# Memory handed over with its features on the partitions, no identity turns ahead of the first product, and the first two weight panels advanced together by contraction tiles

## The chip, the cores and the metric

The kernel runs on one core of a Trainium2 chip. The metric is device time in microseconds (us) of that core, for one execution of the whole block. The engines are named as in the profile: PE multiplies matrices, ACT, DVE and POOL work element by element, SP issues most transfers (DMAs).

## The reference, cut to what matters

The block normalises an input `x` (512 tokens, 1024 features) and runs three mixer branches. Only the opening of the third, the attention into 256 memory tokens, and what lies beside it are touched here:

```python
mem_h = rms_norm(mem, mem_norm_g[l])            # mem: 256 tokens x 1024 features
kv_m = mem_h @ w_mem_kv[l]                      # 1024 x 2048, four panels of 512 columns
km = rms_norm(kv_m[..., :D_MEM].reshape(B, -1, MEM_HEADS, MEM_HD), mem_k_norm_g[l])
vm = kv_m[..., D_MEM:].reshape(B, -1, MEM_HEADS, MEM_HD)
...
h = rms_norm(x, norm_g[l])
proj = h @ w_in[l]
```

All of it is fp32; a product needs its contraction (the features) on the partitions.

## The kernel before, in words

Every fp32 operand is split into a high part (rounded) and a low part (the rest), and each product is three matmuls: high by high, high by low, low by high. ACT makes the high parts (`w_hi`, `memT_hi`), DVE the low parts (`w_lo`, `memT_lo`), PE multiplies. Three engines thus follow each other for each weight piece: `piece_high` (L1234) on ACT, `piece_low` (L1859) on DVE, `first_products` (L780) on PE.

The opening works on panels 0 and 1 of `w_mem_kv`, each 8 contraction tiles (k = 0 to 7, 128 rows each) by 512 columns, for two memory tiles m of 128 tokens: 2 x 2 x 8 x 3 = 96 matmuls of 512 columns, into four PSUM banks `proj0` to `proj3`. `w_raw`, `w_hi` and `w_lo` hold two halves (kh 0 and 1) of four contraction tiles. `PIECES` (L26) cuts the loads: panel 0's tiles 0 to 3 one by one (pieces 0 to 3), panel 1's tiles 0 to 3 in two pairs (4, 5), panel 0's tiles 4 to 7 in two pairs (6, 7, into the same place as pieces 0 to 3). The rest comes by `load_kv_half` (L434). Pieces 6 and 7 wait on SP for `w_lo_done` 1, the low part of piece 3, and on ACT for `w_used` 1, the last product of the tiles that they replace.

The memory comes with tokens on partitions (`load_mem`, L452, four transfers of 256 KB). PE turns each half of a memory tile with the identity (`turn_tile`, L663, four turns of 128 x 128), ACT writes the high part out of PSUM times the gain (`mem_high`, L1209) and DVE the low part (`mem_low`, L1833). The gain is loaded as rows on ACT's queue and turned too (L777). `warm` (L769) fills PE's start with identity turns. A product of a memory tile waits for the tile's turn and split, so `first_products` takes one panel and one memory tile after the other in an order written out by hand (L793 to L815).

The sums of squares of the memory come from ACT's `square` (L1197) with an accumulating output; `variance` on DVE and a power on POOL (L2544) make 1/rms, and `kv_evac` (L1265) applies it when ACT takes the banks out of PSUM. After panels 0 and 1 PE runs panel 2 (`kv_panel`, L746) into banks 0 and 1, with the turns of `x` between its products, then a turn of 92 rows of small vectors (`vector_transposes`, L684), then the rest of the block. SP's queue is one list: pieces, then `load_kv_half` with the four tiles of `x` between, then small vectors, then `w_in`.

Each engine takes its instructions in the order written; a wait holds all that stands behind it on that engine.

Of the kernel before, what the change touches and what calls it, by code (L numbers as in the profile page):

```python
# [7 lines left out]
F32 = mybir.dt.float32  # L8
# [6 lines left out]
P = 128  # L15
# [13 lines left out]
FIRST_BANKS = ((0, 1), (2, 3))  # L29
WARM_TURNS = (8, 7)  # L30
# [111 lines left out]
def hybrid_block(nc, x, mem, positions, norm_g, mem_norm_g, w_in, conv_w, conv_b, mlstm_gate_b,  # L142
                 mlstm_norm_g, dsa_q_norm_g, dsa_k_norm_g, mem_q_norm_g, mem_k_norm_g,
                 w_mem_kv, w_branch, w_out, inv_freq, pos_cols, w_idx2, out):
    ctx = ExitStack()
    with ctx:
# [44 lines left out]
        mem_in = merged[:, 0:MT * D].rearrange("p (t n) -> p t n", t=MT)  # L191
        g_row = arena[:, 0:D]
        memg_rows = arena[0:KT, D:D + P]
        memg_col = cols[:, 0:KT]
        x_sc = arena[:, 2 * D:4 * D].rearrange("p (b n) -> p b n", b=2)
        junk = arena[:, 4 * D:5 * D]
        idx2_raw = arena[:, 8 * D - KT * I_COLS:8 * D].rearrange("p (k n) -> p k n", k=KT)
        vec_rows = arena[0:92, 5 * D:5 * D + P]
# [130 lines left out]
        mem_landed = [sem(f"mem_landed{n}") for n in range(2 * MT)]  # L329
        g_landed, memg_landed = sem("g_landed"), sem("memg_landed")  # L330
        mem_hi = sem("mem_hi")
        half_turned, half_hi, half_lo = sem("half_turned"), sem("half_hi"), sem("half_lo")
# [52 lines left out]
        vec_cols = sem("vec_cols")  # L385
        memg_cols = sem("memg_cols")
# [9 lines left out]
        def turn_bank(n, k):  # L396

            return att[FIRST_BANKS[n][k // 2] if n < MT else TURN_BANK[n]]

        def half_tile(n):  # L400

            return (n % 2, n // 2) if n < 2 * MT else (n // 2, n % 2)

# [4 lines left out]
        wi, wkv, wo = w_in[0], w_mem_kv[0], w_out[0]  # L408
# [15 lines left out]
        def _(sp):  # L424
# [9 lines left out]
            def load_kv_half(n, p, c0, kh):  # L434

                for i, free, landed in ((0, (w_first_lo, n + 4), piece_landed[n]), (1, (w_lo_done, p * 2 + kh - 1), w_landed[kh])):
                    sp.wait_ge(*free)
                    rows = slice(kh * S + i * 256, kh * S + (i + 1) * 256)
                    sp.dma_start(w_raw[:, kh, 2 * i:2 * i + 2], wkv[rows, c0:c0 + 512].rearrange("(k p) n -> p k n", p=P))\
                        .then_inc(landed, 16)  # L440
# [38 lines left out]
            load_kv_half(0, KV_PANEL[1], 512, 1)  # L479
            load_x(X_TILES[:2])  # L480
# [2204 lines left out]
```

## Time and profile before

| | |
|---|---|
| median of 3 runs | 976.26 us (976.03 to 976.55) |
| span of the profiled execution | 974.9 us |
| busy share of the span: PE, DVE, ACT, POOL | 100%, 67%, 53%, 25% |
| moved by DMA | 103.36 MB |

A timeline row is: start (us from the span's start), duration, engine, line, operation, output<-inputs, shape, count of merged instructions, and in brackets the idle time of the engine ahead of it with what ended it. Matmul ends are modelled and overlap the next start, so the distance of starts tells the pace. A row of the windows gives, for a stretch, the busy time and count of each engine, the granted clock, the mean busy share of the DMA engines and what they moved in GB/s.

### The profile page before, as it was taken

Reading aid. Unit: us, or ns where it says so; the run is one execution under the profiler, and the core shown is the slowest. Engines: PE = TensorE matmul, PEld = TensorE weight load, DVE = VectorE, ACT = ScalarE, POOL = GpSimd, SP = SyncE. Lnnn points to the kernel's source line nnn. Section 1 sums busy time; section 2 is a strip of 40 time slices with the busy share of each in tenths; the row PEclk is TensorE's granted clock in tenths of the full one; section 3 lists DMA queues with packets and bytes.
Section 4 is the critical chain, followed back from the end, with each engine's and each line's share of the span. In section 5 each row is a group of like instructions: output and inputs, shape, how many; then the busy total and the mean of one; then the engine's idle time right before and its main releaser. Section 6 shows DMA issues by size and latency. Waiting matters only on the chain.

```text
span 974.9 us, 13868 instructions
## 1 busy us (share of the span) xinstructions
PE 970.7 (100%) x4993; PEld 857.5 (88%) x4993; DVE 649.9 (67%) x1047; ACT 518.5 (53%) x790; POOL 246.0 (25%) x167
## 2 busy tenths in 40 slices
PE   9999999999999999999999999999999999999998
PEld 7888888898989989989898888898998989988887
DVE  6878987779565564653756443796776867735486
ACT  6977644445453453544447211776675857741351
POOL 0100822121011010010110800271622626106600
DMA  8624222112332322332322342707024050638412
GB/s 277 242 87 130 87 87 76 45 54 68 95 97 65 97 65 78 84 95 66 97 87 87 87 129 76 237 12 213 4 80 146 31 153 1 229 94 302 153 43 87
DMA packets 111622, 103.36 MB, mean 106 GB/s; under 512 B 4468, under 2 KB 95192, under 8 KB 111196
## 3 DMA queue, kind: packets, MB, share of 16 engines
q1 hardware_dynamic: 111564, 102.80, 33.5%
q8 instruction: 26, 0.43, 0.2%
q14 instruction: 16, 0.13, 0.0%
q10 hardware_dynamic: 16, 0.00, 0.0%
HBM read 98.59 MB, written 4.20 MB: 105 GB/s over the span
## 4 chain that ended last, share of the span: by engine, by line
PE 100%; POOL 0%; issue 0%; DVE 0%; POOLq 0%
PE proj L619 59%; PE proj L1064 9%; PE att L1091 7%; PE proj L1091 5%; PE att L1141 3%; PE proj L789 2%; PE att L946 2%; PE att L964 2%; PE att L886 1%; PE att L908 1%; PE proj L1021 1%; PE att L954 1%; PE att L935 1%; PE att L679 1%; PE att L1021 1%; PE proj L1141 1%
## 5 line engine op out<-in xcount | busy, mean ns | idle before, releaser
L1807 DVE TENSOR_TENSOR w_lo<-w_raw,w_hi 128x1536 fp32r<-128x1536 f32 (+1 forms) x58 | 124.0, 2138 | 134.8 <-ACT w_hi L1191 129.5
L1191 ACT ACTIVATE w_hi<-w_raw 128x1536 fp32r<-128x1536 f32 (+1 forms) x58 | 97.4, 1680 | 147.9 <-PE proj L619 147.7
L619 PE MATMUL proj<-hT_hi,w_hi 128*128 128x512 f32 x384 | 150.2, 391 | 0.0
L619 PE MATMUL proj<-hT_hi,w_lo 128*128 128x512 f32 x384 | 149.8, 390 | 0.0
L619 PE MATMUL proj<-hT_lo,w_hi 128*128 128x512 f32 x384 | 149.6, 390 | 0.0
L619 PE MATMUL proj<-w_hi,hT_hi 128*128 128x384 f32 (+1 forms) x280 | 96.7, 345 | 0.0
L619 PE MATMUL proj<-w_hi,hT_lo 128*128 128x384 f32 (+1 forms) x280 | 95.3, 340 | 0.0
L619 PE MATMUL proj<-w_lo,hT_hi 128*128 128x384 f32 (+1 forms) x280 | 95.1, 340 | 0.0
L619 PEld LDWEIGHTS proj<-hT_hi,w_lo 128*128 128x128 f32 x384 | 72.1, 188 | 15.2
L619 PEld LDWEIGHTS proj<-hT_lo,w_hi 128*128 128x128 f32 x384 | 72.1, 188 | 14.5
L619 PEld LDWEIGHTS proj<-hT_hi,w_hi 128*128 128x128 f32 x384 | 72.1, 188 | 14.5
L619 PE MATMUL proj<-y_hi,w_hi 128*128 128x512 f32 x192 | 75.4, 393 | 0.0
L619 PE MATMUL proj<-y_lo,w_hi 128*128 128x512 f32 x192 | 74.8, 389 | 0.0
L619 PE MATMUL proj<-y_hi,w_lo 128*128 128x512 f32 x192 | 74.7, 389 | 0.0
L2574 POOL TENSOR_TENSOR arena<-arena 128x1024 f32<-128x1024 f32 x8 | 15.2, 1896 | 229.9 <-ACT arena L1466 229.9
L619 PEld LDWEIGHTS proj<-w_hi,hT_hi 128*128 128x128 f32 x280 | 52.6, 188 | 1.4
L619 PEld LDWEIGHTS proj<-w_lo,hT_hi 128*128 128x128 f32 x280 | 52.6, 188 | 1.4
L619 PEld LDWEIGHTS proj<-w_hi,hT_lo 128*128 128x128 f32 x280 | 52.5, 188 | 1.0
L2299 DVE TENSOR_TENSOR w_lo<-w_raw,w_hi 128x1536 fp32r<-128x1536 f32 (+1 forms) x21 | 35.3, 1682 | 23.4 <-ACT w_hi L1593 23.4
L2605 POOL TENSOR_TENSOR w_raw<-merged,w_raw 128x384 f32<-128x384 f32 x32 | 41.9, 1351 | 29.8 <-DVE w_lo L2299 29.8
L1593 ACT ACTIVATE w_hi<-w_raw 128x1536 fp32r<-128x1536 f32 (+1 forms) x21 | 29.1, 1387 | 31.4 <-POOL w_raw L2605 12.9
L619 PEld LDWEIGHTS proj<-y_hi,w_lo 128*128 128x128 f32 x192 | 36.0, 188 | 7.5
(445 smaller groups left out, 2399.3 us busy)
## 6 DMA issues: line engine op xcount, KB each, us to landing
w_raw<-w_in_in SPq DMA_DIRECT2D x106, 256.0 KB, 3.2
w_raw<-w_in_in SPq DMA_DIRECT2D x32, 512.0 KB, 4.4
w_raw<-w_in_in SPq DMA_DIRECT2D x6, 1024.0 KB, 5.3
w_raw<-w_mem_kv_in SPq DMA_DIRECT2D x10, 512.0 KB, 7.2
yF<-x_in SPq DMA_DIRECT2D x8, 512.0 KB, 7.9
w_raw<-w_branch_in SPq DMA_DIRECT2D x16, 256.0 KB, 3.5
w_raw<-w_branch_in SPq DMA_DIRECT2D x4, 1024.0 KB, 6.4
w_raw<-w_branch_in SPq DMA_DIRECT2D x8, 512.0 KB, 5.5
```

The costliest lines, as they stand in the source:

```text
L619: ins = mm(ps, lhs[a](k, k0), rhs[b](k, k0), start=(first and k == 0 and j == 0), stop=(last and k == KH - 1 and j == 2))
L789: ins = mm(banks[2 * c + m][:, :], memT[a][:, k, m * P:(m + 1) * P], (w_hi, w_lo)[b][:, c, k % KH, :], start=(k == 0 and j == 0), stop=(k ...
L946: ins = mm(att[(t + 2) % 4][:, 0:(t + 1) * P], b_qT[a][:, t * P:(t + 1) * P], b_kT[b][:, 0:(t + 1) * P], start=(j == 0), stop=(j == 2))
L964: ins = mm(att[2][:, s * P:S], v[:, s, :], b_pT[p][:, 4 * s * P:(3 * s + TT) * P], start=(s == 0 and j == 0), stop=(s == TT - 1 and j == 2))
L1064: ins = mm(banks[b][:, :], w[a][:, k, e * P:(e + 1) * P], hT[b_][:, kh * KH + k, :], start=(kh == 0 and k == 0 and j == 0), stop=(kh == 1 ...
L1091: ins = mm(to[t][:, 0:UNIT_N], lhs[a](k, t), w[b][:, k, :], start=(start and k == 0 and j == 0), stop=(k == KH - 1 and j == 2), skip_group ...
L1141: ins = mm(to[t][:, :], lhs[a](k, t), w[b][:, k, :], start=(start and k == 0 and (a, b) == (0, 0)), stop=(k == KH - 1 and (a, b) == parts[ ...
L1191: A_(w_hi[:, kh, :, 0:n], w_raw[:, kh, :, 0:n], ACT.Copy).then_inc(w_hi_done, 1)
L1593: A_(operand(op_hi, n), raw_of(n, first), ACT.Copy).then_inc(op_high, 1)
L1807: V.tensor_tensor(w_lo[:, kh, :, 0:n], w_raw[:, kh, :, 0:n], w_hi[:, kh, :, 0:n].bitcast(F32), ALU.subtract).then_inc(w_lo_done, 1)
L2299: V.tensor_tensor(operand(op_lo, n), raw_of(n, first), operand(op_hi, n).bitcast(F32), ALU.subtract)\
L2605: ins = G.tensor_tensor(dst[:, at], left[:, at], right[:, at], ALU.subtract)
```

## The change

- The host hands the memory over transposed, gain in front: `mem_t` is 128 partitions x (8 gains + 8 tiles x 256 tokens). Its first two contraction tiles are loaded on ACT's queue (132 and 128 KB), tiles 2 and 3 (256 KB) and 4 to 7 (512 KB) on SP's. `w_mem_kv` is handed over with each partition's rows of a panel in one piece, and the small vectors as columns (one load in place of five, no turn of them on PE).
- PE's turns of the memory and of the gain are gone. PE starts with one product of a constant tile and 14 identity turns. `mem_high` and `mem_low` work on one contraction tile of 256 tokens at a time, out of SBUF.
- `first_products` takes both memory tiles, and panels 0 and 1 advance together: one tile of each, the next tile of each, then pairs. The pieces are loaded in that order; piece 4 is now panel 0's tiles 2 and 3, and its low part is the `w_lo_done` 1 for which SP's load of piece 6 waits. One tile of `x` is queued ahead of that wait.
- Features lie on partitions now, so the sum of squares over features is a sum over partitions: ACT squares the memory in two parts (`mem_square`) after piece 7, POOL adds 2048 values per partition down to 256 in three steps, PE sums over the partitions with two one-column products (`mem_row_totals`), DVE and POOL make 1/rms of both memory tiles at once.

```diff
-TURN_BANK = (0, 1, 0, 1, 2, 3, 0, 1, 2, 3, 0, 1)
-PIECES = ((0, 0, 1), (0, 1, 2), (0, 2, 3), (0, 3, 4), (1, 0, 2), (1, 2, 4), (0, 0, 2), (0, 2, 4))
-LAST_PIECES = {3: 16, 5: 16, 7: 32}
+TURN_BANK = (2, 3, 0, 1, 2, 3, 0, 1)
+MEM_PIECES = ((0, 1), (1, 2), (2, 4), (4, 8))
+PIECES = ((0, 0, 1), (1, 0, 1), (0, 1, 2), (1, 1, 2), (0, 2, 4), (1, 2, 4), (0, 0, 2), (0, 2, 4))
+LAST_PIECES = {4: 16, 5: 16, 7: 32}
...
             load_piece(0, 0, 0)
-            load_mem(1)
-            load_piece(1, 0, 0)
+            load_piece(1, 0, 1)
             load_piece(2, 0, 0)
-            load_piece(3, 0, 0)
-            load_piece(4, 0, 512)
+            load_piece(3, 0, 1)
             load_mem(2)
-            load_piece(5, 0, 512)
+            load_piece(4, 0, 0)
+            load_piece(5, 0, 1)
             load_mem(3)
+            load_x(X_TILES[:1])
             sp.wait_ge(w_lo_done, 1)
             load_piece(6, 1, 0)
             load_piece(7, 1, 0)
...
+            def mem_row_totals():
+                pe.wait_ge(mem_summed, 1)
+                for m in range(MT):
+                    ins = mm(att[1][:, m:m + 1], mem_sq[:, m * P:(m + 1) * P], ones[:, :], start=True, stop=True)
+                ins.then_inc(mem_totals, 1)
...
+            pe.wait_ge(warm_set, 1)
+            mm(att[3][:, 0:P], warm_src, warm_src, start=True, stop=True)
             pe.wait_ge(ident_set, 1)
-            warm(WARM_TURNS[0])
-            pe.wait_ge(memg_landed, 16)
-            turn(att[2][:, 0:KT], memg_rows, ident[0:KT, 0:KT]).then_inc(memg_cols, 1)
-            turn_tile(0)
-            warm(WARM_TURNS[1])
+            warm(WARM_TURNS)
...
+            first_products(0, 0, 1, (w_first_cast, 1), (w_first_lo, 1), 1)
+            first_products(1, 0, 1, (w_first_hi, 1), (w_first_lo, 2), 1)
+            first_products(0, 1, 2, (w_first_hi, 2), (w_first_lo, 3), 2)
+            first_products(1, 1, 2, (w_first_hi, 3), (w_first_lo, 4), 2)
+            first_products(0, 2, 4, (w_hi_done, 1), (w_lo_done, 1), 4).then_inc(w_used, 1)
+            first_products(1, 2, 4, (w_hi_done, 2), (w_lo_done, 2), 4).then_inc(w_used, 1)
+            first_products(0, 4, 6, (w_first_hi, 4), (w_first_lo, 5), 6)
+            first_products(0, 6, 8, (w_hi_done, 3), (w_lo_done, 3), 8, (proj_done[0], proj_done[1]))
+            mem_row_totals()
+            first_products(1, 4, 6, (w_first_hi, 5), (w_first_lo, 6), 6)
+            first_products(1, 6, 8, (w_hi_done, 4), (w_lo_done, 4), 8, (proj_done[2], proj_done[3]))
...
+            act.dma_start(mem_in[:, 0:KT + MEM], mem_t[:, 0:KT + MEM]).then_inc(mem_landed[0], 16)
+            act.dma_start(mem_in[:, KT + MEM:KT + 2 * MEM], mem_t[:, KT + MEM:KT + 2 * MEM]).then_inc(mem_landed[1], 16)
...
             piece_high(6)
             piece_high(7)
-            square(0)
+            mem_square(0)
+            mem_square(1)
             half_high(1, 0, 2, (w_used, 2))
-            square(1)
             square(2)
             square(3)
...
             half_low(1, 0, 1)
-            variance(0)
-            variance(1)
+            mem_variance()
...
+            pool.wait_ge(mem_squared, 2)
+            steps.then(G.tensor_tensor(mem_sq[:, 0:D], mem_sq[:, 0:D], mem_sq[:, D:2 * D], ALU.add))
+            steps.then(G.tensor_tensor(mem_sq[:, 0:512], mem_sq[:, 0:512], mem_sq[:, 512:D], ALU.add))
+            G.tensor_tensor(mem_sq[:, 0:256], mem_sq[:, 0:256], mem_sq[:, 256:512], ALU.add).then_inc(mem_summed, 1)
```

PE before, in the second half of panels 0 and 1 (tiles 4 to 7): `proj0` and `proj1` are panel 0 for the two memory tiles, `proj2` is panel 1.

```order
L789 MATMUL proj0<-w_lo,y_hi 128x512 [waits w_lo_done]
L789 MATMUL proj0<-w_lo,y_hi 128x512
L789 MATMUL proj1<-w_hi,y_hi 128x512 [waits xT_lo]
L789 MATMUL proj1<-w_hi,y_lo 128x512 x4
L789 MATMUL proj1<-w_lo,y_hi 128x512 x4
L789 MATMUL proj2<-w_hi,y_hi 128x512 [waits w_first_hi]
```

PE now, at the same place, from the products of piece 7's low part on:

```order
L766 MATMUL proj0<-w_lo,y_hi 128x512 [waits w_lo_done,mem_high_of]
L766 MATMUL proj1<-w_lo,y_hi 128x512 x2
L766 MATMUL proj0<-w_hi,y_lo 128x512 [waits mem_low_of]
L766 MATMUL proj1<-w_hi,y_lo 128x512 x2
L665 MATMUL att1<-ones,arena 128x1 [waits mem_summed]
L665 MATMUL att1<-ones,arena 128x1
L766 MATMUL proj2<-w_hi,y_hi 128x512 [waits w_first_hi,mem_high_of]
```

Between panel 0's last product and panel 1's next one PE now has two one-column products that wait for POOL (`mem_summed`).

POOL before, from its opening on (`ident` and `causal` are constants, the rest is the power for 1/rms):

```order
L2533 MEMSET ident 128x128
L2534 AFFINE_SELECT ident<-ident 128x128
L2536 MEMSET causal 128x128
L2537 AFFINE_SELECT causal<-causal 128x128 [waits pool_step]
L2544 TENSOR_TENSOR small<-small,minus_half 128x1 [waits x_var,consts]
L2544 TENSOR_TENSOR small<-small,minus_half 128x1 [waits x_var] x5
```

POOL now, behind the same constants:

```order
L2483 AFFINE_SELECT causal<-causal 128x128 [waits pool_step]
L2489 TENSOR_TENSOR arena<-arena 128x1024 [waits mem_squared,consts]
L2490 TENSOR_TENSOR arena<-arena 128x512 [waits pool_step]
L2491 TENSOR_TENSOR arena<-arena 128x256 [waits pool_step]
L2493 TENSOR_TENSOR small<-small,minus_half 128x2 [waits x_var]
L2496 TENSOR_TENSOR small<-small,minus_half 128x1 [waits x_var] x4
```

Three additions, each waiting for the one before, stand ahead of the powers; the first waits for both squares of ACT.

DVE now, between piece 6 and the variance of the memory (L1815 are the low parts of pieces 6 and 7, L1828 those of panel 1's tiles 4 to 7):

```order
L1815 TENSOR_TENSOR w_lo<-w_raw,w_hi 128x1024 [waits w_first_hi]
L1815 TENSOR_TENSOR w_lo<-w_raw,w_hi 128x1024 [waits w_hi_done]
L1849 CAST small<-small 128x4 [waits ang_landed]
L1851 TENSOR_TENSOR arena<-arena,small 128x256 [waits dve_step]
L1853 TENSOR_SCALAR arena<-arena 128x256 [waits dve_step]
L1828 TENSOR_TENSOR w_lo<-w_raw,w_hi 128x1024 [waits w_first_hi,dve_step]
L1828 TENSOR_TENSOR w_lo<-w_raw,w_hi 128x1024 [waits w_hi_done]
L1785 TENSOR_SCALAR small<-att 128x2 [waits mem_totals]
```

Its order is that of before; the last row took the place of two single variances, and it waits for PE's totals where those waited for ACT.

## Rows read from the trace of the kernel before

**Rows 1.** The page: busy time of PE, and PE's 40 slices.
```profile
PE 970.7 (100%) x4993; PEld 857.5 (88%) x4993; DVE 649.9 (67%) x1047; ACT 518.5 (53%) x790; POOL 246.0 (25%) x167
PE   9999999999999999999999999999999999999998
```
**Rows 2.** Timeline of PE, start: identity turns and first products.
```profile
1.54 1.97 PE L772 MATMUL att<-ident 128*128 128x128 f32 x8 [1.54 <-POOL ident L2534]
...
5.97 0.78 PE L789 MATMUL proj<-w_hi,y_hi 128*128 128x512 f32 x1
6.54 0.63 PE L789 MATMUL proj<-w_lo,y_hi 128*128 128x512 f32 x1
6.97 0.63 PE L789 MATMUL proj<-w_hi,y_lo 128*128 128x512 f32 x1
```
**Rows 3.** Timeline of PE: panel 1's last 24 products, panel 2, the vectors' turn.
```profile
25.15 0.62 PE L789 MATMUL proj<-w_hi,y_hi 128*128 128x512 f32 x2
...
30.59 0.39 PE L619 MATMUL proj<-w_hi,y_hi 128*128 128x512 f32 x1
...
45.07 0.24 PE L687 MATMUL att<-ident,arena 92*128 92x92 f32 x1
45.38 0.43 PE L619 MATMUL proj<-hT_hi,y_hi 128*80 128x512 f32 x1
```
**Rows 4.** The windows: four stretches of the opening.
```profile
2.00:9.00 7.00, 7.00 (x30) 5.75 (x29) 3.31 (x10) 3.59 (x11) 0.08 (x1) 1.00 0.80 246
9.00:12.00 3.00, 3.00 (x14) 2.44 (x13) 1.99 (x6) 1.35 (x3) 0.00 (x0) 1.00 1.02 366
12.00:15.00 3.00, 3.00 (x16) 2.21 (x15) 1.37 (x2) 1.95 (x2) 0.00 (x0) 1.00 0.71 206
20.00:30.00 10.00, 10.00 (x46) 8.28 (x45) 8.72 (x20) 8.55 (x14) 3.23 (x4) 1.00 1.02 398
```
**Rows 5.** Timeline of ACT: high parts of pieces 4, 6 and 7, first square.
```profile
12.20 1.06 ACT L1242 ACTIVATE w_hi<-w_raw 128x1024 fp32r<-128x1024 f32 x1 [0.78 <-DMA w_raw<-w_mem_kv_in]
...
17.09 1.11 ACT L1242 ACTIVATE w_hi<-w_raw 128x1024 fp32r<-128x1024 f32 x1
18.36 1.06 ACT L1242 ACTIVATE w_hi<-w_raw 128x1024 fp32r<-128x1024 f32 x1 [0.16 <-DMA w_raw<-w_mem_kv_in]
19.32 1.04 ACT L1207 ACTIVATE arena<-merged 128x1024 f32<-128x1024 f32 x1
```
**Rows 6.** Timeline of DVE: low parts of pieces 3 and 4.
```profile
11.45 0.69 DVE L1865 TENSOR_TENSOR w_lo<-w_raw,w_hi 128x512 fp32r<-128x512 f32 x1 [1.01 <-ACT w_hi L1242]
13.29 1.23 DVE L1865 TENSOR_TENSOR w_lo<-w_raw,w_hi 128x1024 fp32r<-128x1024 f32 x1 [1.15 <-ACT w_hi L1242]
```
**Rows 7.** Timeline of all engines: SP's queue issues pieces 6 and 7.
```profile
12.17 0.89 SPq L459 DMA_DIRECT2D w_raw<-w_mem_kv_in  x2
```
**Rows 8.** Timeline of POOL: additions and subtractions of two SBUF operands.
```profile
111.64 1.30 POOL L2561 TENSOR_TENSOR arena<-arena 128x512 f32<-128x512 f32 x1 [0.18 <-ACT arena L1415]
112.89 4.47 POOL L2562 TENSOR_TENSOR y_hi<-yF,m_qh 128x1024 fp32r<-128x1024 f32 x1
...
140.14 2.41 POOL L2562 TENSOR_TENSOR y_hi<-yF,m_qh 128x1024 fp32r<-128x1024 f32 x1
...
553.74 2.40 POOL L2592 TENSOR_TENSOR arena<-arena 128x1024 f32<-128x1024 f32 x1
```
**Rows 9.** Timeline of DVE at two of those times.
```profile
112.81 2.29 DVE L1807 TENSOR_TENSOR w_lo<-w_raw,w_hi 128x2048 fp32r<-128x2048 f32 x1
...
547.05 4.36 DVE L1807 TENSOR_TENSOR w_lo<-w_raw,w_hi 128x2048 fp32r<-128x2048 f32 x1
```
**Rows 10.** Lines by shape, DVE, 0 to 50 us: low parts of two tiles.
```profile
L1878 DVE TENSOR_TENSOR w_lo<-w_raw,w_hi 128x1024 fp32r<-128x1024 f32 x6 | 7.2, 1224 | 1.4 <-ACT w_hi L1252 0.8 <-ACT w_hi L1254 0.5
```
**Rows 11.** Timeline of all engines: variance, power, evacuation of banks 0 and 1.
```profile
24.91 0.21 DVE L1822 TENSOR_SCALAR small<-small 128x1 f32<-128x1 f32 x2
25.21 1.19 POOL L2544 TENSOR_TENSOR small<-small,minus_half 128x1 f32<-128x1 f32 x2 [23.14 <-DVE small L1822]
...
29.13 1.25 ACT L1271 ACTIVATE merged<-proj,small 128x512 f32<-128x512 f32 x2
```

More of the change, by code:

```diff
@@ L496, in _ @@
             load(IDX_PANEL, [(wi, C_QI, 512)])
-            load(KV_PANEL[3], [(wkv, 3 * 512, 512)])
+            for kh in range(2):
+                sp.wait_ge(w_lo_done, KV_PANEL[3] * 2 + (kh - 1))
+                sp.dma_start(w_raw[:, kh], w_kv[:, 3, kh * KH:(kh + 1) * KH]).then_inc(w_landed[kh], 16)
             with sp.Fori(0, M_HEADS) as h:
@@ L772, in warm @@
                     turn(att[3][:, 0:P], ident[:, :], ident[:, :])
+            pe.wait_ge(warm_set, 1)
+            mm(att[3][:, 0:P], warm_src, warm_src, start=True, stop=True)
             pe.wait_ge(ident_set, 1)
-            warm(WARM_TURNS[0])
-            pe.wait_ge(memg_landed, 16)
-            turn(att[2][:, 0:KT], memg_rows, ident[0:KT, 0:KT]).then_inc(memg_cols, 1)
-            turn_tile(0)
-            warm(WARM_TURNS[1])
-            def first_products(c, m, k0, k1, high=(), low=(), mem_low=(), weights_last=True):
-                orders = (((0, 0), high), ((1, 0), mem_low), ((0, 1), low))
-                if not weights_last:
-                    orders = (orders[0], orders[2], orders[1])
-                for j, ((a, b), wait) in enumerate(orders):
-                    if wait:
-                        pe.wait_ge(*wait)
-                    for k in range(k0, k1):
-                        ins = mm(banks[2 * c + m][:, :], memT[a][:, k, m * P:(m + 1) * P], (w_hi, w_lo)[b][:, c, k % KH, :],
-                                 start=(k == 0 and j == 0), stop=(k == KT - 1 and j == 2))
-                return ins
@@ new lines, in first_products @@
+            def first_products(c, k0, k1, high, low, mem_ready, done=()):
+                for j, (a, b, wait) in enumerate(((0, 0, high), (0, 1, low), (1, 0, None))):
+                    pe.wait_ge(mem_low_of if a else mem_high_of, mem_ready)
+                    if wait is not None:
+                        pe.wait_ge(*wait)
+                    for m in range(MT):
+                        for k in range(k0, k1):
+                            ins = mm(banks[2 * c + m][:, :], memT[a][:, k, m * P:(m + 1) * P], (w_hi, w_lo)[b][:, c, k % KH, :],
+                                     start=(k == 0 and j == 0), stop=(k == KT - 1 and j == 2))
+                        if done and j == 2:
+                            ins.then_inc(done[m], 1)
+                return ins
@@ new lines, in square, with mem_square @@
+                act.wait_ge(x_landed[X_TILES[i - MT]], 16)
+                if i > MT:
+                    act.wait_ge(x_ssq, i - MT)
+                A_(junk, x_in[:, X_TILES[i - MT]], ACT.Square, accum_out=xss[:, i:i + 1]).then_inc(x_ssq, 1)
+            def mem_square(half):
+                for n in ((0, 1, 2), (3,))[half]:
+                    act.wait_ge(mem_landed[n], 16)
+                A_(mem_sq[:, half * D:(half + 1) * D].rearrange("p (k n) -> p k n", k=KH),
+                   memT_raw[:, half * KH:(half + 1) * KH], ACT.Square).then_inc(mem_squared, 1)
@@ L1286, in _ @@
             piece_high(3)
+            mem_high(2)
+            mem_high(3)
             piece_high(4)
             piece_high(5)
-            mem_high(2)
-            mem_high(3)
+            for k in range(KH, KT):
+                mem_high(k)
             piece_high(6)
             piece_high(7)
-            square(0)
+            mem_square(0)
+            mem_square(1)
             half_high(1, 0, 2, (w_used, 2))
-            square(1)
             square(2)
@@ L1892, in _ @@
             piece_low(3)
+            mem_low(2)
+            mem_low(3)
             piece_low(4)
             piece_low(5)
-            mem_low(2)
-            mem_low(3)
+            for k in range(KH, KT):
+                mem_low(k)
             piece_low(6)
```

270 lines of the change are left out of this document (96 added, 174 removed).

## The prediction

> **What bounds the kernel now.** I read the page first: PE is busy for 970.7 of 974.9 us, and its first slice of 24 us is as full as the others [rows 1]. So a change of this opening counts only by the moment at which PE can go on with the work that is the same in both kernels; nothing later is idle and could absorb a delay. That work is the last 24 products of panel 1 (its tiles 4 to 7), then panel 2 and the rest. In PE's timeline they start at 25.15 and panel 2 at 30.59, so 24 products take 5.44 us or 0.227 each, the 2.4 GHz level; the first products stand 0.43 apart (6.54 to 6.97), the 1.2 GHz level [rows 2, 3]. I then read the windows for what the loads reach [rows 4], and ACT, DVE, SP and POOL around the pieces and the sums [rows 5 to 11]. The sum below is for one number, the start of those 24 products now, against 25.15. The profiled run has a span of 974.9 us and the median of the runs is 976.26; I keep the 1.3 us outside the span.
>
> **What is removed.** The turns of the memory and the gain stand between products. Without them the first product can start behind 14 turns of 1.97/8 = 0.246 us from 1.54 on, at 4.98 at the earliest, instead of 5.97 [rows 2]. 72 products stand ahead of the last 24. With 6 at 0.43 and 66 at 0.227 they take 17.6 us, and PE would come to the 24 products at about 22.5 if nothing else made it wait: a gain of 2.65 us at the most. The vectors' turn costs 45.07 to 45.38, 0.31 us [rows 3]; it goes whatever else happens, since the columns come by a load long before they are used.
>
> **What is added: a wait in PE's order.** The two one-column products of the totals stand between panel 0's last product and panel 1's next. PE takes its work in order, so the 24 products, panel 2 and all behind them are queued behind a wait for POOL, which waits for ACT's squares, which stand behind the high part of piece 7 on ACT. Call the start of that high part L7 (18.36 in before [rows 5]). From there:
> - ACT: the high part holds ACT 0.96 (18.36 to 19.32), two squares take 0.96 and 1.04: 2.95 us [rows 5].
> - POOL: 1024 columns 2.40, 512 columns 1.30; for 256 no row exists, and half of the step from 512 to 1024 taken off 1.30 gives 0.75 as an estimate: 4.45 us [rows 8].
> - Three hand-overs between engines and the waits between POOL's steps 0.3, the two narrow products 0.2 (estimates; the vectors' turn took 0.31 [rows 3]).
>
> That is L7 + 7.9 us. POOL, however, doesn't run beside DVE here. The subtraction of two SBUF operands over 1024 columns takes 2.41 us on POOL alone and 4.47 when DVE's subtraction (2.29 us) began 0.08 us ahead of it; the other way round DVE's took 4.36 where POOL's 2.40 us addition was running [rows 8, 9]. One waits for the whole of the other. The Trainium skill, "SBUF — State Buffer", section "Who interferes with whom", says the same of a two-input DVE operation and GpSimd, and the trace agrees (4.47 for 2.41). In the new order of DVE the low parts of panel 1's tiles 4 to 7, two of 1.22 us [rows 10], become ready behind the squares, while POOL adds. If each takes its turn between two additions, POOL's chain grows by 2.44 to **L7 + 10.35**.
>
> **When L7 comes.** SP may load piece 6 only when piece 4's low part is done; before it was piece 3's. As many bytes stand ahead of piece 4 as ahead of it before (2052 against 2048 KB), so it may land near 12.2, where ACT took it [rows 5]. Its high part (1.06) and low part (1.23) then end at 14.5 [rows 5, 6], and SP issues pieces 6 and 7 at 14.55 instead of 12.17 [rows 7]. From the issue to the high part of piece 7 before went 18.36 - 12.17 = 6.2 us: upper end 20.7. Lower end: at the 398 GB/s of 20 to 30 us from 2 us on [rows 4], the 4.72 MB up to piece 7 would be there at 13.9; but ACT may write tiles 4 to 7 only after the 36th product, 4.98 + 2.6 + 30 x 0.227 = 14.4, and piece 6's high part stands ahead: 15.3. I take **18.4**, as before. The reason is the hole at 12 to 15 us: 206 GB/s where 398 are possible, so some 576 KB weren't moved while SP waited [rows 4]. The tile of `x` queued ahead of the wait (512 KB) fills just that, so piece 7's end moves little. Rows of the weights and the memory that are longer in DRAM may lift the 246 GB/s of 2 to 9 us [rows 4]; that counts to the lower end.
>
> **The sum.** With L7 at 18.4, piece 7's low part ends at 20.7 and 8 products of 0.227 behind it end panel 0 at 22.5. The squares end at 21.35, the additions at about 28.3, the totals at 28.75. PE stands idle for 6 us, and the 24 products start at 28.75 instead of 25.15: +3.6; less 0.31 for the vectors' turn: +3.3. 976.26 + 3.3 = **979.6 us** (span 978.2).
>
> **What costs nothing.** Behind the totals the variance, the power and the two evacuations (0.21, 1.19, 1.25 us [rows 11]) run beside the 24 products (5.44 us); without that cover panel 2 would wait for banks 0 and 1, up to 2.7 us. The `mem_high` and `mem_low` steps are fewer and wider than before, on engines that wait for loads at that time; if they delayed a piece they would move L7 within its bounds. The other two squares, the later loads of `x` and panel 2 go into the time at 398 GB/s in which PE has its 24 products and panel 2 ahead of it; the one load of columns replaces five.
>
> **The rivals.**
> - **The clock falls in the wait.** Before, the first products ran at the lower level although PE had been turning since 1.54, and reached 0.227 only behind 6.97 [rows 2]: coming out of no work costs some 5.4 us of lower level. After 6 us of nothing the 24 products may do so again. If it lasts 3.4 us (8 products) that is 8 x 0.2 = 1.6 us, if it lasts 6 us (14 products) 2.8: about 981.8. Against it speaks only that no row of before shows an idle PE in the middle, and that the idle time is shorter if the lock bites less. The Trainium skill, "TensorE: Matmul & The Clock Gate", section "Why this matters for your kernels", says that pauses between bursts of matmuls bring the half clock back; no row here shows it.
> - **Early pieces, lock as taken** (L7 15.3 to 17.4): the 24 products at 25.65 to 27.75, 976.5 to 978.6.
> - **The lock doesn't bite** (DVE's low parts come late, for lack of their weights, or early, before the additions), L7 as taken: 26.3, +1.15 - 0.31, about 977.1.
> - **Early pieces and no lock: faster.** This is the other side. The mechanism is the loads: four first pieces in the order in which they are used, and two queues, so that L7 comes near 15.3. Then the totals are there at 23.2, and the gain of the removed turns stays: 23.2 - 25.15 - 0.31 = -2.3, 974.0; at best 22.5, which gives 973.3. It decides for faster below L7 = 15.6 and needs DVE out of POOL's way; against it speaks the rate of 246 GB/s [rows 4].
> - **Late pieces** (L7 19.4 to 20.7, lock): 980.6 to 981.9.
>
> **How the numbers follow.** A measurement of this kernel can tell 0.2%, or 1.95 us, from no change: faster is below 974.3, slower above 978.2. Chances: the forecast (L7 17.4 to 19.4, lock, clock kept, 978.6 to 980.6) 0.29; the clock falls (980.6 to 983.0) 0.23; early pieces with lock 0.17, of which 0.03 above 978.2; no lock 0.11; early and no lock (973.3 to 975.7) 0.13, of which 0.09 below 974.3; late 0.07. Slower: 0.29 + 0.23 + 0.07 + 0.03 = 0.62. Faster: 0.09. Within: 0.29. The range leaves out the lower half of the faster case and the upper part of the clock's case: 974.5 to 982.6.
>
> **What would show it.** On PE, an idle time of 3 to 6 us that POOL's last addition ends, ahead of the two narrow products: right; none, and the 24 products at about 22.5: the wait is hidden and the forecast is wrong. On ACT, the start of piece 7's high part tells L7. On POOL, additions of 2.4, 1.3 and 0.75 us mean no lock; 2.5 or 3.6 for one of the last two with a low part on DVE beside it means lock. The distance of the 24 products behind the wait (0.43 or 0.227) tells the clock. In the windows 12 to 15 us must show no hole. The distance from the start of panel 2 to the end must be as before, less 0.31; if it isn't, the effect lies where I didn't look.

## The result, and the profile after

| | before | changed |
|---|---|---|
| median of 16 runs | 976.36 us (975.91 to 977.28) | 978.78 us (977.34 to 981.29) |
| span of the profiled execution | 974.9 us | 978.4 us |

The ratio is 1.0025 with a 95% interval of 1.0018 to 1.0032: slower by 1.8 to 3.1 us. The runs of the changed kernel fall into two groups by the granted clock that each run lists: six at 1.000 with times of 977.3 to 978.2 (median 977.8), ten at 0.997 or 0.998 with 978.5 to 981.3 (median 979.3). The profiled execution is one of the ten.

PE is busy for 971.9 us (99%) where it was 970.7 (100%) [rows 1]. Its timeline at the places of [rows 2, 3] (start, duration, operation, count, and in brackets the idle time ahead of it with what ended it):

```profile
5.88 1.22 PE L766 MATMUL proj<-w_hi,y_hi 128*128 128x512 f32 x2 [1.04 <-ACT y_hi L1181]
6.90 1.05 PE L766 MATMUL proj<-w_lo,y_hi 128*128 128x512 f32 x2
...
10.29 0.63 PE L766 MATMUL proj<-w_hi,y_lo 128*128 128x512 f32 x2
...
23.48 1.07 PE L766 MATMUL proj<-w_hi,y_lo 128*128 128x512 f32 x4
26.17 0.61 PE L665 MATMUL att<-ones,arena 128*128 128x1 f32 x4 [1.62 <-POOL arena L2491]
26.63 1.47 PE L766 MATMUL proj<-w_hi,y_hi 128*128 128x512 f32 x4
27.90 1.91 PE L766 MATMUL proj<-w_lo,y_hi 128*128 128x512 f32 x4
29.61 1.61 PE L766 MATMUL proj<-w_hi,y_lo 128*128 128x512 f32 x4
31.05 1.09 PE L766 MATMUL proj<-w_hi,y_hi 128*128 128x512 f32 x4
...
33.81 0.39 PE L606 MATMUL proj<-w_hi,y_hi 128*128 128x512 f32 x1
```

The first product starts at 5.88, no earlier than before (5.97 [rows 2]), behind 1.04 us of idle time, and products stay some 0.43 apart until 10.3. Panel 0's last group starts at 23.48 and has four products of 0.227, so PE is through at 24.39. Then it waits for POOL (L2491 is the last addition), and the 24 products start at 26.63 instead of 25.15: 1.48 us. They take 33.81 - 26.63 = 7.18 us instead of 5.44: another 1.74. They lie in the first twelve, which take 31.05 - 26.63 = 4.42 us where 2.72 are usual; the four of 27.90 stand 0.43 apart, the lower level. Together panel 2 starts 3.22 us later than before.

The other engines on that path:

```profile
11.94 0.80 SPq L445 DMA_DIRECT2D w_raw<-w_mem_kv_in  x2
...
16.48 2.01 ACT L1197 ACTIVATE w_hi<-w_raw 128x1024 fp32r<-128x1024 f32 x2 [2.56 <-PE proj L766]
...
18.40 2.00 ACT L1174 ACTIVATE arena<-merged 128x1024 f32<-128x1024 f32 x2
...
20.55 2.52 POOL L2489 TENSOR_TENSOR arena<-arena 128x1024 f32<-128x1024 f32 x1 [18.48 <-ACT arena L1174]
...
20.84 2.38 DVE L1854 TENSOR_SCALAR arena<-arena 128x256 f32<-128x256 f32 x1
...
23.14 1.30 POOL L2490 TENSOR_TENSOR arena<-arena 128x512 f32<-128x512 f32 x1
23.26 3.94 DVE L1828 TENSOR_TENSOR w_lo<-w_raw,w_hi 128x1024 fp32r<-128x1024 f32 x2
...
24.53 1.59 POOL L2491 TENSOR_TENSOR arena<-arena 128x256 f32<-128x256 f32 x1
...
28.26 1.26 ACT L1226 ACTIVATE merged<-proj,small 128x512 f32<-128x512 f32 x2 [0.81 <-POOL small L2493]
```

SP issues pieces 6 and 7 at 11.94 (12.17 in [rows 7]). The high parts of both are one row: they start at 16.48, when PE has used the tiles that they replace, so piece 7's starts at about 17.4. The squares end at 20.4, the additions at 26.12.

The windows (us, PE, PEld, DVE, ACT, POOL busy, granted clock, DMA share, GB/s), to be read against [rows 4]:

```profile
2.00:9.00 7.00, 5.96 (x21) 4.92 (x20) 3.73 (x8) 4.45 (x9) 0.07 (x1) 1.00 0.95 307
9.00:12.00 3.00, 3.00 (x12) 2.39 (x11) 2.13 (x5) 2.40 (x3) 0.00 (x0) 1.00 1.03 415
12.00:15.00 3.00, 3.00 (x15) 2.49 (x14) 2.77 (x5) 1.71 (x4) 0.00 (x0) 1.00 0.89 266
24.00:31.00 7.00, 5.38 (x19) 4.06 (x18) 6.83 (x13) 6.07 (x10) 3.88 (x4) 0.76 0.92 314
```

The loads move 307 GB/s from 2 to 9 us instead of 246, and the hole at 12 to 15 is smaller (266 against 206). From 24 to 31 the granted clock is 0.76; it was 1.00 in every stretch of [rows 4]. The column also gives 1.00 from 2 to 9 us, here and in [rows 4], where the first products stand 0.43 apart. It doesn't show such a start, so the level there is read from the distance alone.

### The profile page after: what moved, and what is told of

Its sections match the earlier page's. It is cut to its first block, busy times and chain, and to the rows that moved or that the text cites. A ratio compares the mean times of both kernels' runs of the same rounds, so it can differ in the third digit from the quotient of the medians.

```text
span 978.4 us, 13835 instructions
## 1 busy us (share of the span) xinstructions
PE 971.9 (99%) x4980; PEld 858.1 (88%) x4980; DVE 653.3 (67%) x1037; ACT 517.2 (53%) x780; POOL 251.4 (26%) x169
## 4 chain that ended last, share of the span: by engine, by line
PE 98%; POOL 1%; DMA 0%; ACT 0%; issue 0%; DVE 0%; ACTq 0%; POOLq 0%
PE proj L606 58%; PE proj L1030 9%; PE att L1057 7%; PE proj L1057 5%; PE att L1107 3%; PE proj L766 2%; PE att L912 2%; PE att L930 2%; PE att L852 1%; PE att L874 1%; PE proj L987 1%; PE att L920 1%; PE att L901 1%; PE att L987 1%; PE proj L1107 1%; PE att L1000 0%
```

## The experiments

Each is the changed kernel with one edit unless it says more, so it is to be compared with 978.78. All were run beside the kernel before on the same chip, whose median there lay between 976.32 and 976.47.

**The clock alone.** PE gets turns to do in the wait; the wait stays.

```
             first_products(0, 6, 8, (w_hi_done, 3), (w_lo_done, 3), 8, (proj_done[0], proj_done[1]))
+            warm(18)
             mem_row_totals()
```

> The changed kernel with 18 identity turns (some 0.09 us each at the upper level, 1.6 us) on PE between panel 0's last product and the wait for POOL's sums; the wait itself stays. Theory (the clock falls because PE stands idle there): the 24 products behind the wait run at 0.227 us, granted clock 1.000 in all runs, and the time is that of the changed kernel's undisturbed runs, 977.3 to 978.2, median 977.8. Rival (the clock falls there whatever PE does, or the turns don't count as work): still 0.998 in most runs, 978.8 us.

Measured: 978.08 us (977.40 to 978.46), ratio to before 1.0018 (1.0009 to 1.0027), granted clock 1.000 in all 11 runs. PE, POOL and the window:

```profile
22.85 2.13 PE L751 MATMUL att<-ident 128*128 128x128 f32 x18
25.50 1.17 PE L766 MATMUL proj<-w_hi,y_hi 128*128 128x512 f32 x4
...
31.56 0.47 PE L606 MATMUL proj<-w_hi,y_hi 128*128 128x512 f32 x1 [0.24 <-DVE w_lo L1829]
...
24.24 0.73 POOL L2492 TENSOR_TENSOR arena<-arena 128x256 f32<-128x256 f32 x1
...
22.00:31.00 9.00, 8.95 (x51) 7.32 (x49) 8.69 (x17) 8.36 (x11) 4.33 (x5) 1.00 0.97 345
```

The clock no longer falls, and the runs lie where the changed kernel's six runs at 1.000 lie (the expectation calls them undisturbed). So the fall of the clock behind the wait comes from PE's idle time, and it is worth the distance between the two groups, some 1.5 us, in those runs that have it. What is left, 1.4 to 1.7 us over before, is there without it.

That rest isn't PE's wait for the sums alone. In this trace the sums are there at 24.97 and the 24 products start at 25.50, only 0.35 us later than before; but panel 2 starts at 31.56, 0.97 later, behind a wait for DVE's low parts. DVE is late mainly because POOL's additions hold it. Its rows in this trace, and last the row of the kernel before for panel 2's low parts:

```profile
20.19 2.38 DVE L1850 CAST small<-small 128x4 f32<-128x4 int32 x1 [0.83 <-DMA arena<-inv_freq_in]
...
23.06 1.26 DVE L1854 TENSOR_SCALAR arena<-arena 128x256 f32<-128x256 f32 x1
...
30.20 2.35 DVE L1829 TENSOR_TENSOR w_lo<-w_raw,w_hi 128x1024 fp32r<-128x1024 f32 x2
...
28.25 2.36 DVE L1878 TENSOR_TENSOR w_lo<-w_raw,w_hi 128x1024 fp32r<-128x1024 f32 x2 [0.43 <-ACT w_hi L1252]
```

The same cast and step take 0.17 and 0.29 us in `sums_on_dve` below, where POOL doesn't add. No run moves only this hold away, so its share isn't measured.

**More of the lock.** DVE's low parts come while POOL adds.

```
             piece_low(7)
+            half_low(1, 0, 1)
             dve.wait_ge(ang_landed, 16 * 2)
...
-            half_low(1, 0, 1)
             mem_variance()
```

> The changed kernel with DVE's low parts of panel 1's tiles 4 to 7 moved ahead of the four small steps on the angles, so that they are ready while POOL adds. Theory (a DVE operation of two SBUF operands and POOL's addition exclude each other): each of the two low parts takes its turn between two additions; POOL's sums end at 27.3 to 28.5 instead of 26.1, 1.2 to 2.4 us later, 980.0 to 981.2 us. Rival (what delayed the last addition was something else): additions of 2.5, 1.3 and 0.6 to 0.75 us, sums at 25.3, 978 us or less.

Measured: 981.67 us (980.38 to 981.92), ratio 1.0051 (1.0037 to 1.0064), clock 0.997 or 0.998 in all 5 runs.

```profile
20.41 2.41 POOL L2489 TENSOR_TENSOR arena<-arena 128x1024 f32<-128x1024 f32 x1 [18.34 <-ACT arena L1174]
22.89 2.13 POOL L2490 TENSOR_TENSOR arena<-arena 128x512 f32<-128x512 f32 x1
25.10 1.58 POOL L2491 TENSOR_TENSOR arena<-arena 128x256 f32<-128x256 f32 x1
...
26.74 1.02 PE L665 MATMUL att<-ones,arena 128*128 128x1 f32 x4 [3.44 <-POOL arena L2491]
27.62 2.05 PE L766 MATMUL proj<-w_hi,y_hi 128*128 128x512 f32 x4
...
35.40 0.39 PE L606 MATMUL proj<-w_hi,y_hi 128*128 128x512 f32 x1
```

The additions take 6.12 us in all; 2.40, 1.30 and 0.73 [rows 8, and the row of fill_wait above] make 4.43 without DVE beside them. The lock costs 1.7 us here, by its direction as expected. But the sums end at 26.68, only 0.56 us later than in the changed kernel's trace and not 1.2 to 2.4, because the lock had cost 1.0 there already. From trace to trace panel 2 starts 1.6 us later (35.40 for 33.81): 1.0 by the later start of the 24 products (27.62 for 26.63), since the two narrow products run at the lower level too, and 0.6 by a longer stretch at that level. The median is above the expected 980.0 to 981.2. It rises by 2.9 us, and by 2.4 against the changed kernel's ten runs at the lower clock; that the clock falls in every run now is a part of this, and the rest isn't shown.

**The wait away, first way.** The sums go to DVE.

```
+            dve.wait_ge(mem_squared, 2)
+            then(V.tensor_tensor(mem_sq[:, 0:D], mem_sq[:, 0:D], mem_sq[:, D:2 * D], ALU.add))
+            then(V.tensor_tensor(mem_sq[:, 0:512], mem_sq[:, 0:512], mem_sq[:, 512:D], ALU.add))
+            V.tensor_tensor(mem_sq[:, 0:256], mem_sq[:, 0:256], mem_sq[:, 256:512], ALU.add).then_inc(mem_summed, 1)
             half_low(1, 0, 1)
...
-            pool.wait_ge(mem_squared, 2)
-            steps.then(G.tensor_tensor(mem_sq[:, 0:D], mem_sq[:, 0:D], mem_sq[:, D:2 * D], ALU.add))
-            steps.then(G.tensor_tensor(mem_sq[:, 0:512], mem_sq[:, 0:512], mem_sq[:, 512:D], ALU.add))
-            G.tensor_tensor(mem_sq[:, 0:256], mem_sq[:, 0:256], mem_sq[:, 256:512], ALU.add).then_inc(mem_summed, 1)
```

> The changed kernel with the three additions on DVE (1.23, 0.69 and some 0.48 us), ahead of the low parts of panel 1's tiles 4 to 7, in place of POOL. Theory (wait and lock): the sums are there at some 23.1, ahead of panel 0's last product at 24.4; PE doesn't stand idle, granted clock 1.000, panel 2 at 29.9 to 30.3: 975.0 to 975.6 us. Rival (DVE is late then): its low parts end 1 to 2 us later and panel 1's products wait for them instead, 976.5 to 978 us.

Measured: 976.19 us (975.86 to 976.51), ratio 0.9998 (0.9989 to 1.0007), clock 1.000 in all 11 runs.

```profile
23.27 0.61 PE L665 MATMUL att<-ones,arena 128*128 128x1 f32 x4 [0.27 <-DVE arena L1858]
...
29.53 0.47 PE L606 MATMUL proj<-w_hi,y_hi 128*128 128x512 f32 x1
...
28.17 2.35 DVE L1828 TENSOR_TENSOR w_lo<-w_raw,w_hi 128x1024 fp32r<-128x1024 f32 x2
...
44.45 0.43 PE L606 MATMUL proj<-hT_hi,y_hi 128*80 128x512 f32 x1 [0.16 <-DVE hT_lo L1806]
```

With the sums off POOL the whole loss is gone: 2.6 us. The edit takes away PE's wait and POOL's hold on DVE together (panel 2's low parts start at 28.17 again), so it doesn't tell the two apart. And the time is that of before, not the 975.0 to 975.6 of the theory. Panel 2 starts 1.06 us earlier than before and the vectors' turn is gone, yet the first product with `x` starts at 44.45 instead of 45.38: of 1.37 us 0.93 are left, and PE waits there for the low part of `x`'s last turned half. At the end of the span 0.5 are left (974.4 for 974.9).

**The wait away, second way.** The totals go behind half of the 24 products.

```
-            mem_row_totals()
             first_products(1, 4, 6, (w_first_hi, 5), (w_first_lo, 6), 6)
+            mem_row_totals()
```

> The changed kernel with the two one-column products of the totals moved on PE behind panel 1's products of tiles 4 and 5 (12 products, 2.7 us); nothing else. Theory (the loss is the wait for POOL in PE's order, 1.5 us, and the lower clock behind it, 1.7 us): PE has work until 27.1, POOL's sums are there at 26.1, so there is no idle time ahead of panel 1's products, the granted clock stays 1.000, and panel 2 starts at 30.1 to 30.5 instead of 33.8: 975.1 to 975.8 us. Rival (the loss is that the pieces come later, and the wait only shows it): panel 1's products wait for their weights instead, 978 to 979 us.

Measured: 978.78 us (978.27 to 980.10), ratio 1.0026 (1.0015 to 1.0036), clock 1.000 in 7 of 8 runs.

```profile
25.68 1.17 PE L766 MATMUL proj<-w_lo,y_hi 128*128 128x512 f32 x4 [0.22 <-DVE w_lo L1828]
...
32.27 0.47 PE L606 MATMUL proj<-w_hi,y_hi 128*128 128x512 f32 x1 [1.29 <-DVE w_lo L1828]
...
28.14 0.16 DVE L1785 TENSOR_SCALAR small<-att 128x2 f32<-128x2 f32 x1 [0.93 <-PE att L665]
```

The theory fell: PE doesn't wait for the totals and the clock holds, but panel 2 waits 1.29 us for its low parts, and the loss stays. The rival had the time (978 to 979) but not the place; it named panel 1's products, which wait 0.22 us. Panel 2's low parts stand on DVE behind the step that reads the totals (L1785), ahead of which DVE now stood idle for 0.93 us: the wait went from PE's order into DVE's, which POOL's additions had held up besides (L1854 takes 2.38 us in this trace too). To see whether that is all, DVE's step was moved behind the angle steps:

```
             half_low(1, 0, 1)
-            mem_variance()
...
+            mem_variance()
             variance(2)
```

> The totals behind panel 1's products of tiles 4 and 5 on PE, as in the run totals_later, and DVE's step on them moved behind the rest of the angle steps. Theory (in totals_later DVE's step took over the wait and held up the angles, the variances of x and panel 2's low parts behind it): DVE no longer stands idle ahead of that step, panel 2's low parts come about 0.9 us earlier, its first product starts at 31.0 to 31.6 instead of 32.3: 977.4 to 978.1 us. Rival (the evacuation of banks 0 and 1, later by then, holds panel 2): no better than totals_later, 978.5 to 979.3 us.

Measured: 979.43 us (979.11 to 980.18), ratio 1.0034 (1.0022 to 1.0046).

```profile
32.26 0.50 PE L606 MATMUL proj<-w_hi,y_hi 128*128 128x512 f32 x1 [1.53 <-ACT merged L1226]
```

The rival was right. DVE doesn't stand idle any more, but now ACT's evacuation of banks 0 and 1, which needs the totals, holds panel 2 for 1.53 us. So the totals can't be asked for later either: behind them hang DVE's queue and the two banks.

**The gain side.** Four edits of the start and the loads.

```
-WARM_TURNS = 14
+WARM_TURNS = 17
```

> The changed kernel with 17 identity turns ahead of the first product instead of 14 (to about 5.6 instead of 4.84), so that PE doesn't stand idle for up to 1 us before it. Theory (POOL's sums set the end of the wait, and an idle PE is what sets the clock back): the first products run 0.23 to 0.33 apart in all runs, panel 0 ends near 22.7 instead of 24.2, but the sums still end at 25.0 to 26.1; the wait grows to 2.5 to 3.5 us and the clock falls behind it in most runs: 978.5 to 980.5 us, no gain. Rival (the slow start is what costs): 1.3 to 1.6 us less, 977.2 to 977.5 us.

Measured: 978.98 us (977.82 to 982.08), ratio 1.0029 (1.0016 to 1.0041), clock below 1.000 in 4 of 7 runs. In its trace products run at the upper level from 5.54 on but for the first, panel 0 is through at 23.2, and PE waits:

```profile
25.96 0.74 PE L665 MATMUL att<-ones,arena 128*128 128x1 f32 x4 [2.65 <-POOL arena L2491]
```

As the theory said: what the start wins the wait takes back, because the sums hardly come earlier (they end at 25.91 for 26.12).

```
-            act.dma_start(mem_in[:, 0:KT + MEM], mem_t[:, 0:KT + MEM]).then_inc(mem_landed[0], 16)
...
+            load_mem(0)
             load_piece(0, 0, 0)
```

> The changed kernel with the memory's first tile at the head of SP's queue, as in the kernel before, instead of on ACT's queue beside the weights. Theory (the first product is late because the first tile now shares the transfers with four pieces): it lands near 3.7 instead of 5.2 and the first product starts at 5.0 to 5.3 instead of 5.4 to 5.9; the gain ends in the wait for the sums, 978.3 to 980.5 us. Rival (the two queues side by side are no loss, or the weight piece becomes the late one): first product at 5.4 or later, time the same.

Measured: 979.29 us (977.76 to 982.27), ratio 1.0031 (1.0021 to 1.0042).

```profile
5.65 0.43 DVE L1832 CAST w_hi<-w_raw 128x512 fp32r<-128x512 f32 x1 [4.62 <-DMA w_raw<-w_mem_kv_in]
...
6.22 0.70 PE L767 MATMUL proj<-w_hi,y_hi 128*128 128x512 f32 x2 [1.66 <-DVE w_hi L1832]
...
25.84 0.61 PE L666 MATMUL att<-ones,arena 128*128 128x1 f32 x4 [1.16 <-POOL arena L2491]
...
2.00:9.00 7.00, 5.32 (x22) 4.33 (x21) 3.32 (x7) 3.25 (x7) 0.07 (x1) 0.90 0.95 299
9.00:12.00 3.00, 3.00 (x10) 2.37 (x10) 1.95 (x4) 2.45 (x4) 0.00 (x0) 0.67 1.02 418
```

The theory fell here: ACT splits the memory's tile at 4.97, which lies among the times of the traces that load it as the changed kernel does (4.29 to 5.32), but now the first weight piece is what is late, and the first product starts at 6.22. In these traces one or the other of the transfers under way together is the last. In this one the clock falls at the start (0.90 and 0.67) and holds behind the wait for the sums (1.00 from 24 to 33 us).

```
-            load_x(X_TILES[:1])
             sp.wait_ge(w_lo_done, 1)
...
-            load_x(X_TILES[1:2])
+            load_x(X_TILES[:2])
```

> The changed kernel with the first tile of x loaded where the kernel before had it (behind panel 1's second half), no longer ahead of SP's wait. Theory (that tile fills a hole in the transfers that the wait leaves, and piece 7 then waits for the earlier products or its own issue): piece 7's high part starts within 0.5 us of 17.4, 12 to 15 us show about 200 GB/s, and the time is within 0.7 us of 978.8. Rival (its 512 KB hold up pieces 6 and 7): piece 7's high part 1.3 us earlier, near 16.1, and 977.0 to 977.6 us.

Measured: 979.32 us (977.88 to 981.59), ratio 1.0028 (1.0016 to 1.0040).

```profile
17.70 1.06 ACT L1196 ACTIVATE w_hi<-w_raw 128x1024 fp32r<-128x1024 f32 x1 [0.86 <-DMA w_raw<-w_mem_kv_in]
...
12.00:15.00 3.00, 3.00 (x15) 2.38 (x14) 2.82 (x6) 1.75 (x5) 0.00 (x0) 1.00 0.66 178
```

As the theory said: piece 7's high part starts at 17.70 and the hole is back (178 GB/s). The tile of `x` costs nothing where the change put it.

```
+        def kv_rows(c, k0, k1):
+            return w_kv[k0 * P:k1 * P, c * 512:(c + 1) * 512].rearrange("(k p) n -> p k n", p=P)
...
-                sp.dma_start(w_raw[:, kh, k0:k1, :], w_kv[:, c, half * KH + k0:half * KH + k1])\
+                sp.dma_start(w_raw[:, kh, k0:k1, :], kv_rows(c, half * KH + k0, half * KH + k1))\
```

> The changed kernel with the weights of the memory in their first layout (rows of 512 columns, 2 KB each, also where a load brings two tiles or more). Theory (longer rows move more per us): 9 to 12 us show some 366 GB/s instead of 415, piece 7's high part starts 0.3 to 1 us later, and the time is 0.3 to 1 us above the changed kernel's 978.8. Rival (the rate is that of the queue, not of the rows): the rate and the time as in the changed kernel.

Measured: 980.56 us (979.07 to 982.51), ratio 1.0040 (1.0027 to 1.0053), 5 runs.

```profile
18.32 1.06 ACT L1202 ACTIVATE w_hi<-w_raw 128x1024 fp32r<-128x1024 f32 x1 [0.30 <-DMA w_raw<-w_mem_kv_in]
...
9.00:12.00 3.00, 2.83 (x11) 2.08 (x12) 1.80 (x4) 2.12 (x4) 0.00 (x0) 1.00 1.05 417
```

Half right. Piece 7 comes 0.9 us later and the time rises, by more than expected; but the rate at 9 to 12 us is the same as in the changed kernel (417 against 415), so it is not there that the longer rows help. From 2 to 9 us it is 281, where the traces with the longer rows and the changed kernel's order of loads have 307 to 314. How the 1.8 us are made up stays open; the run's trace has a first product as early as 4.85, so single traces differ at the start by more than this.

**What is late next.** `dve_first` is `sums_on_dve` with 17 turns and with the sums, panel 1's last low parts and the variance ahead of all angle steps; `dve_first_x` loads the last tile of `x` ahead of panel 2's second half; `dve_low_early` is `dve_first` with this edit on DVE:

```
+            variance(2)
+            variance(3)
+            half_low(0, 1, 2)
...
-            variance(2)
-            variance(3)
-            half_low(0, 1, 2)
             x_scale(2)
```

> The three additions on DVE as in sums_on_dve, but directly behind piece 7's low part, ahead of the angle steps, with panel 1's last low parts and the variance behind them, and 17 turns at the start. Theory (the gain of the removed turns shows once nothing waits for the sums): panel 0's last product is followed by panel 1 without idle time, panel 2 starts at 28.6 to 29.3 instead of 29.5, 975.2 to 976.0 us. Rival (x's last tile is the next thing late: in sums_on_dve PE already waited 0.16 us for its low part at 44.5): PE waits there for what was won, and the time stays at 976.0 to 976.4 us.

> As dve_first, with the last tile of x loaded ahead of panel 2's second half. If x's last tile is what is late next, the wait ahead of the first product with x goes and the time is 0.2 to 0.6 us below dve_first; if panel 2's second half becomes late by its 1.3 us instead, PE waits there and the time is that of dve_first or up to 1 us more.

> As dve_first, with the variances of x's first two tiles and the low parts of panel 2's first half moved on DVE ahead of the last seven angle steps. Theory (in dve_first PE's wait of 1.2 us ahead of panel 2 is DVE's order: those low parts stood behind the angles): panel 2 starts at 28.6 to 29.2 instead of 30.2, and of that 1 to 1.5 us as much comes through as x's tiles allow: 975.4 to 976.1 us. Rival (x's scaled tiles and their low parts, now behind the angles, or the later sines on ACT, take its place): PE waits in panel 2 or ahead of the first product with x, 976.3 to 977.0 us.

Measured: `dve_first` 976.61 us (ratio 1.0002, 0.9993 to 1.0011), `dve_first_x` 976.97 (1.0007, 0.9998 to 1.0016), `dve_low_early` 977.11 (1.0006, 0.9997 to 1.0015). In `dve_first` the totals follow panel 0 at 22.93 without a wait, and PE stops at panel 2, which neither its theory nor its rival had named. In `dve_first_x` its second case came: panel 2's second half is later on DVE (34.20 instead of 33.52), `x`'s parts with it, and the first product with `x` starts at 46.18 where `dve_first` has it at 44.95. In `dve_low_early` panel 2 runs (its first product at 28.82, where before's stood at 30.59), and PE stops at `x` instead, twice. First the row of `dve_first`:

```profile
30.22 0.47 PE L606 MATMUL proj<-w_hi,y_hi 128*128 128x512 f32 x1 [1.20 <-DVE w_lo L1828]
```

and the rows of `dve_low_early`:

```profile
28.82 0.39 PE L606 MATMUL proj<-w_hi,y_hi 128*128 128x512 f32 x1
...
32.39 1.09 PE L658 MATMUL att<-ident,arena 128*128 128x128 f32 x8 [0.69 <-DVE arena L1793]
...
44.88 0.44 PE L606 MATMUL proj<-hT_hi,y_hi 128*80 128x512 f32 x1 [0.50 <-DVE hT_lo L1806]
```

Its theory was right on panel 2 and its rival on the place where PE stops; the time is 0.1 us above the rival's. `x`'s scaled tile (L1793) and its last low part (L1806) come hardly earlier than in `dve_first` (31.06 for 31.13, 44.05 for 44.12). None of the three kernels is measurably faster than before.

## Why the prediction was right, and where its steps were not

The time, the sign and the range held: 978.78 against 979.6, in 974.5 to 982.6. The cause that the forecast put first, POOL's sums, is shown: with the sums elsewhere the loss goes (sums_on_dve), and PE's wait for them in its own order is in the trace, at 1.62 us and not the 3 to 6 that the prediction gave as its sign. But the agreement to 0.8 us is luck in part: a wait taken too long stands for a fall of the clock that the forecast left to a rival, and for a second way to the loss, over DVE, that it didn't have.

- **The wait** was put at +3.6 us; in the profiled execution it is 1.48, and 0.35 in fill_wait's, which had a quicker start. Its chain in the former: piece 7's high part at 17.4 instead of 18.4; ACT's part 2.96 from there to 20.4, as summed (2.95); POOL 5.41 for the additions, where 4.45 were summed without and 6.89 with the lock. The lock was the right mechanism, its size was wrong by half: 1.0 us instead of 2.44. DVE's low parts came only at 23.26, because DVE had itself been held by POOL's first addition (L1854 took 2.38 us where 0.29 are usual), so one low part stood between two additions and not two. One pairing of rows behind the lock was misread: the addition of 553.74 [rows 8] began after DVE's 4.36 us of 547.05 [rows 9] had ended, at 551.4. Beside it ran two other additions of 1024 columns (L2589, from 544.05 to 549.3), which say the same.
- **DVE's order** is what the prediction left out. It let DVE lengthen POOL's chain, but not POOL hold DVE. Panel 2's low parts start at 30.20 in fill_wait instead of 28.25, and where PE's wait is filled or gone panel 2 waits for them (0.24 us in fill_wait, 1.29 in totals_later). How the 1.4 us of the runs at full clock divide between PE's wait and this isn't shown, since no such run of the changed kernel left a trace.
- **When piece 7 comes** is 17.4 in the profiled execution, at the lower edge of the forecast's case, and loads didn't set it there. SP's later gate wasn't later at all (11.94 instead of the 14.55 of the upper end, because piece 4 was there earlier: ACT took it at 9.59), and ACT waited for PE's 36th product, the mechanism of the lower end, at 16.4 where 14.4 had been worked out; the first product was 0.9 us late and ten products ran at the lower level. In the traces with a quicker start (fill_wait, lows_first, sums_on_dve, warm_more) ACT waited for the loads instead, and piece 7's high part started at 17.0 to 17.3. The reason given for 18.4, the hole that `x` fills, is borne out by x_behind.
- **The gain:** the step that failed is the first product at 4.98. Without turns it starts at 5.88, since the first memory tile, on the second queue beside four pieces, is split only at 5.32; in the other traces with that order of loads it started at 4.85 to 5.86. Panel 0 then ended at 24.4 instead of 22.5, and the idle time was 1.8 us, not 6.
- **The clock:** the forecast kept it; the rival was right in up to ten of sixteen runs, and after a shorter idle time than the rival assumed. In the profiled execution it costs 1.74 us, inside the rival's 1.6 to 2.8, for which two durations had been assumed. That PE's pause brings it is shown by fill_wait: granted clock 1.000 in all 11 runs once PE has turns to do, against 6 of 16. The Trainium skill's row on pauses ("TensorE: Matmul & The Clock Gate", section "Why this matters for your kernels") says the same of a pause between bursts; here a shorter pause than the row gives did it in some runs, and the measurement decides. A mean below 1.000 doesn't tell by itself where the clock fell: in mem_first's trace it fell at the start. So the median is a loss of some 1.4 us at full clock and, in most runs, the clock, some 1.5 us, and not 3.3 us of wait alone.
- **What costs nothing** held in the profiled execution: the two evacuations run at 28.26 to 29.5, and panel 2 starts at 33.81. The prediction didn't look at DVE's queue behind the totals, which makes a later place for the totals no way out (totals_later).
- **The vectors' turn** gives its 0.31 us: the lead of before shrinks from 3.22 us at panel 2 to 2.91 at the first product with `x` (45.38 [rows 3], 48.29 after). From there to the end it grows again by 0.6 (the spans are 978.4 and 974.9), so the prediction's last sign, the same distance from panel 2 to the end less 0.31, fails. The other traces show 0.1 (fill_wait) to 0.6 there as well. Whether that is more than the spread of before's own runs, 975.91 to 977.28, isn't shown. Outside the span lie 1.8 us in each run and not 1.3 (980.16 for the span of 978.4); it changes nothing in the difference.
- **The faster rival** didn't come true even with the sums off POOL: it counted the gain of the removed turns through to the end. Panel 2's low parts and the tiles of `x` are the next things late (dve_first, dve_low_early), which the profile before hid, as PE had no idle time there.

## What to carry to other kernels

Taking work off the busiest engine gains only up to the next thing that is late on its path: look, before summing a gain, at when the operands of the following stage are ready. A reduction that moves from an engine's accumulating output to a chain over three engines turns into a wait at every in-order queue that reads its result, here PE's, DVE's and, by the banks, ACT's evacuation; try each place before choosing one. Look also at what the added work holds up on the engine beside it: POOL's sums made DVE's operands late. And cost an idle time of the matrix engine with the slower products behind it: in the profiled execution they were as dear as the wait (1.74 and 1.48 us).

## What the runs showed of the hardware

- The clock fell behind PE's idle time ahead of the totals, and not in every run: 6 of 16 executions of one kernel kept 1.000. In the traces it fell behind 1.62 us (the changed kernel), 2.65 (warm_more) and 3.44 (lows_first), and held behind 1.16 (mem_first); it also held behind 1.29 us ahead of panel 2 (totals_later). These are single traces, and no limit follows from them. The fall cost 1.7 us in the changed kernel's trace and 2.3 in that of lows_first (7.78 us for the 24 products instead of 5.44).
- What decides the start isn't shown. Where PE stood idle for 1.04 and 1.02 us ahead of the first product (the changed kernel, totals_later), products stayed 0.43 apart until 10.3; with 0.59 to 0.86 us (x_behind, lows_first, sums_on_dve, fill_wait) they ran at 0.23 almost from the first. But in dve_first and in the kernel before they began 0.43 apart with no idle time ahead of them, and in mem_first, after 1.66 us, the clock fell only behind the first products.
- POOL's additions hold up DVE's one-input steps too: the angle step of 0.29 us took 2.38 beside the first addition (L1854, above), and in fill_wait a cast of 0.17 us took 2.38. The prediction counted only with two-input operations. The Trainium skill, "SBUF — State Buffer", section "Who interferes with whom", names `cast` and `tensor_scalar` among the operations that can take the pair of ports shared with GpSimd; the traces agree.
